# Attention with V stationary and P moving, 1/l and gates in a diagonal operand of P's transposes, on one Trainium2 core

## The reference

```python
def rms_norm_2(x, g):
    y = xf * lax.rsqrt(jnp.mean(xf * xf, axis=-1, keepdims=True) + EPS)
    return (y * g.astype(jnp.float32)).astype(x.dtype)
# NSA, one query block of 128
o_cmp = jnp.einsum('bghtn,bngd->btghd', p_cmp.astype(vc.dtype), vc)
o_slc = jnp.einsum('bghtk,bgtkd->btghd', p.astype(vg.dtype), vg)
o_win = jnp.einsum('bghts,bsgd->btghd', p.astype(vw.dtype), vw)
return g[..., 0:1] * o_cmp + g[..., 1:2] * o_slc + g[..., 2:3] * o_win
# fox
s = jnp.einsum('bthd,bshd->bhts', q[:, lo:hi], k[:, :hi]) * scale
s = s + dcum[:, :, lo:hi, None] - dcum[:, :, None, :hi]
p = masked_softmax(s, jnp.arange(hi)[None, :] <= t[:, None])
outs.append(jnp.einsum('bhts,bshd->bthd', p.astype(v.dtype), v[:, :hi]))
```

## Time and profile before

| | us |
|---|---|
| median of 3 runs | 1473.57 (1469.96 to 1474.71) |
| profiled execution | 1473.89 |
| its span, first to last instruction | 1472.0 |
| mean granted TensorE clock | 0.879 of full |

### The profile page before, as it was taken

The page is one execution under the profiler, slowest core; times in us unless marked ns, Lnnn a source line. Parts: engine busy times, 40 slices in busy tenths (PEclk is TensorE's granted clock), DMA queues, the critical chain, the costliest instruction groups (busy, mean ns, idle before and its releaser), DMA issues. The chain is left out here.

```text
span 1472.0 us, 25094 instructions
## 1 busy us (share of the span) xinstructions
PE 1273.8 (87%) x10545; PEld 1181.0 (80%) x10545; DVE 950.6 (65%) x1742; ACT 647.0 (44%) x1144; POOL 109.9 (7%) x131
## 2 busy tenths in 40 slices
PE   3969886889698977969988889998989889999897
PEld 3967785788677866968966789998989768999897
DVE  2886647566965666566776656888555565688852
ACT  2533222455432224465453345665444344566541
POOL 0121000000110000021000100111011000011100
PEclk9989975799999958989985779999899778999989
DMA  6333200234333002324421034554442502455440
GB/s 254 117 118 137 84 2 1 72 133 158 126 115 110 3 1 104 126 86 170 163 79 54 1 118 151 176 174 170 159 154 90 186 29 77 151 173 173 162 169 29
DMA packets 24449, 167.56 MB, mean 114 GB/s; under 512 B 2705, under 2 KB 2833, under 8 KB 8337
## 3 DMA queue, kind: packets, MB, share of 16 engines
q1 hardware_dynamic: 24336, 165.96, 32.3%
HBM read 164.90 MB, written 1.05 MB: 113 GB/s over the span
## 5 line engine op out<-in xcount | busy, mean ns | idle before, releaser
L395 DVE TENSOR_TENSOR WL<-raw,WH 128x1024 fp32r<-128x1024 f32 (+4 forms) x211 | 243.8, 1176 | 161.5 <-ACT WH L382 161.3
L436 PE MATMUL ps<-FR,WH 128*128 128x256 f32 x1156 | 289.8, 289 | 40.8 <-ACT WH L382 25.6
L438 PE MATMUL ps<-FR,WH 128*128 128x256 f32 x1156 | 284.7, 284 | 1.0 <-POOL FR L508 1.0
L382 ACT ACTIVATE WH<-raw 128x1024 fp32r<-128x1024 f32 (+4 forms) x211 | 203.0, 984 | 131.8 <-PE ps L441 65.3
L436 PEld LDWEIGHTS ps<-FR,WH 128*128 128x128 f32 x1156 | 222.6, 193 | 43.5 <-issue 26.6
L438 PEld LDWEIGHTS ps<-FR,WH 128*128 128x128 f32 x1156 | 222.3, 192 | 3.0 <-POOL FR L508 1.5
L436 PE MATMUL ps<-FR,FR 128*128 128x256 f32 x772 | 199.8, 294 | 16.8 <-ACT FR L504 16.8
L438 PE MATMUL ps<-FR,FR 128*128 128x256 f32 x772 | 198.9, 292 | 2.3 <-DVE FR L508 1.4
L395 DVE TENSOR_TENSOR FR<-raw,FR 128x1024 fp32r<-128x1024 f32 (+2 forms) x114 | 133.9, 1194 | 98.4 <-ACT FR L382 98.4
L436 PEld LDWEIGHTS ps<-FR,FR 128*128 128x128 f32 x772 | 152.6, 198 | 20.0 <-ACT FR L504 15.3
L441 PE MATMUL ps<-FR,WL 128*128 128x256 f32 x1156 | 162.5, 283 | 0.5 <-DVE WL L395 0.5
(11 more groups left out here) (313 smaller groups left out, 1878.1 us busy)
## 6 DMA issues: line engine op xcount, KB each, us to landing
raw<-wst_in SPq DMA_DIRECT2D x123, 1024.0 KB, 4.9
raw<-wst_in SPq DMA_DIRECT2D x17, 896.0 KB, 4.6
raw<-wst_in SPq DMA_DIRECT2D x11, 768.0 KB, 4.2
raw<-wst_in SPq DMA_DIRECT2D x4, 912.0 KB, 4.7
cst<-cst_in SPq DMA_DIRECT2D x1, 1681.0 KB, 13.2
X<-xT_in SPq DMA_DIRECT2D x2, 512.0 KB, 4.4
ARENA<-memT_in SPq DMA_DIRECT2D x1, 1024.0 KB, 4.7
out_dram<-X SPq DMA_DIRECT2D x2, 512.0 KB, 2.6
```

What stands on the lines that cost most here:

```text
L382: a.activation(hi[:, 0:cols], src, ACT.Copy).then_inc(*put("split_hi", ("hi", i)))
L395: v.tensor_tensor(lo[:, 0:cols], src, hi[:, 0:cols].bitcast(F32), SUB).then_inc(*put("split_lo", ("lo", i)))
L436: pe.matmul(out, hv[:, k, :], src.hi[:, c, :], start=k0 == 0 and k == ks[0], stop=False)
L438: pe.matmul(out, hv[:, k, :], src.lo[:, c, :], start=False, stop=False)
```

## The change

1. O is computed with V as the stationary operand (64 columns) and transposed P as the moving one (128 columns), so it comes out feature-major. Two jobs fill the two halves of 64 partitions of one bank, alternately.
2. P's transposes become ordinary fp32 matmuls whose moving operand is `dg`, a 128x128 diagonal of 1/l times the gate, one for each head. DVE builds it (reciprocal, gate multiply, tensor_tensor of the identity and the broadcast row), and T waits for it.
3. The outputs are split at once into `w_o`'s operand: ACT writes the high part ("out hi"), DVE the low one. dil and dsa are multiplied into the gate's place `gd`. The 16 transposes of each `w_o` and the turns of the layers go. In NSA a job is one head with its two branches, and the compressed branch is a third term in the same bank; the POOL adds and `cO` go.
4. Squares are summed on POOL (three adds of 128x512), and a norm takes two matmuls instead of eight.
5. One weight slot less (`NMORE` 3). Steps 0, 1, 3, 4 of compress stand ahead of the NSA turns, the rest between the pairs.

```diff
         if s == 2:
-            qpe.wait_ge(*got("exp", j.id))
+            qpe.wait_ge(*got("dg", j.id))
...
-                    ins = pe.transpose(ps[:, 128 * y:128 * y + 128], j.sm[:, i, 128 * kb:128 * kb + 128], ident)
+                    ins = pe.matmul(ps[:, 128 * y:128 * y + 128], j.sm[:, i, 128 * kb:128 * kb + 128], j.dg[:, min(i, j.nl - 1), :],
+                                    start=True, stop=True)
...
                 for kb in range(nkb):
-                    x = i * nkb + kb
-                    ins = pe.matmul(ps[:, 64 * i:64 * i + 64], j.pt[:, 128 * x:128 * x + 128], j.v(i, kb),
-                                    start=kb == 0, stop=kb == nkb - 1)
-            ins.then_inc(*put("attn_pe", ("O", j.id)))
+                    for p, x in zip(HALVES, (j, j.mate)):
+                        t = 128 * (i * nkb + kb)
+                        ins = pe.matmul(ps[p, o:o + 128], x.v(i, kb), x.pt[:, t:t + 128], start=lead and kb == 0, stop=end and kb == nkb - 1)
+            if "gate" in j.more:
+                for p, x in zip(HALVES, (j, j.mate)):
+                    ins = pe.matmul(ps[p, 0:128], x.more["cmp v"], x.more["cmp p"], start=False, stop=True)
+            ins.then_inc(*put("attn_pe", ("O", j.id), ("O", j.mate.id)))
...
+            v.tensor_tensor(j.dg, bc(ident, 1, j.nl), bc(rl, 2, 128), MUL).then_inc(*put("attn_v", ("dg", j.id)))
+            if j.turn == "V":
+                x, n = j.turns[0]
+                to, ps, free = turn_copy(j, x, n)
...
+                v.tensor_copy(to, ps).then_inc(*put("attn_v", ("pt", j.id, x), free))
...
+                hi, lo = (x[:, c0:c0 + j.n_out, t] for x in (j.parts.hi, j.parts.lo))
+                q.wait_ge(*got("out hi", j.id))
+                v.tensor_tensor(lo, po, hi.bitcast(F32), SUB).then_inc(*put("attn_v", free, *[("lo", j.to, c0 + c) for c in range(j.n_out)]))
...
+    def sum_squares(g_, q, tag, sq, steps=(1, 2, 3)):
+
+        for n in steps:
+            q.wait_ge(*got("square", tag, 2 * n))
+            if n > 1:
+                q.wait_ge(*own("square_sum"))
+            g_.tensor_tensor(sq[0], sq[0], sq[n], ADD).then_inc(*put("square_sum", ("summed", tag, 2 * n)))
...
+            chain = [("compress", 2), ("compress", 5), ("compress", 6), ("compress", 7), (1, 0), (0, 0), (1, 1), (0, 1), (1, 2), (0, 2)]
+            self.steps = chain[0:3] + units[0:2] + chain[3:5] + units[2:6] + chain[5:7] + units[6:10] + chain[7:] + units[10:]
```

More of the change, by code:

```diff
@@ L672, in attn_v @@
         if s == 2:
[L673 to L680, removed]
-            q.wait_ge(*got("exp", j.id))
[L682 to L686, removed]
+            rl = j.st[:, 4:4 + j.nl]
+            q.wait_ge(*got("exp", j.id))
+            if j.sm_before is not None:
+                q.wait_ge(*got("sm free", j.sm_before))
+            v.reciprocal(rl, rl).then_inc(*put("attn_v"))
+            q.wait_ge(*own("attn_v"))
             if "gate" in j.more:
-                q.wait_ge(*got("1/l", j.id))
                 q.wait_ge(*got("gates"))
@@ L729, in attn_a @@
                     a.activation(to, ps, ACT.Copy).then_inc(*put("attn_a", ("pt", j.id, x), free))
-        if s == 3 and j.kind == "dil":
+        if s == 3 and j.mate and "times" not in j.more:
             ps, free = psum("O", j.id)
-            q.wait_ge(*got("1/l", j.id))
+            c0 = j.c0
             q.wait_ge(*got("O", j.id))
[L734 to L743, removed]
+            a.activation(j.parts.hi[:, c0:c0 + j.n_out, 128 * j.b:128 * j.b + 128], ps[:, 0:128 * j.n_out].rearrange("p (c q) -> p c q", c=j.n_out),
+                         ACT.Copy).then_inc(*put("attn_a", ("out hi", j.id), *[("hi", j.to, c0 + c) for c in range(j.n_out)]))
     def rope_v(v, q, tag, zt, H, D, half, cname, sname, TA, TB):
@@ L870, in layer_script @@
         dsa = {b: [[("sel", b, i)] for i in range(7)] + [both("dsa", b, s) for s in range(4)] for b in range(2)}
-        dil = [both("dil", b, s) for b in (1, 0) for s in range(4)] + [[("turn dil",)], [("part dil",)]]
+        dil = [both("dil", b, s) for b in (1, 0) for s in range(4)] + [[("part", 5, 3)]]
         lists = [dsa[1], dil, dsa[0]]
@@ L1414, in layer_pe @@
                 if c0 == 0:
[L1415 to L1416 removed]
+                    mean_mm(("in", l), m.sq[0] if l == 0 else lo_[0].sq3[0])
             elif s[0] == "gate":
@@ L1948, in o_v @@
         barrier(q, "V", stage)
-        split_lo(v, q, "w_o", l, 0, ahead=5)
-        for c in range(8):
-            ps, free = psum("oT", l, c)
-            part_lo(v, q, "part_lo_v", m.Y, ("YO", l), c, ps[:, 0:256], free)
         for c0 in range(0, 8, 2):
@@ L1966, in o_a @@
         barrier(q, "A", stage)
-        split_hi(a, q, "w_o", l, 0, ahead=5)
-        for c in range(8):
-            ps, free = psum("oT", l, c)
-            q.wait_ge(*got("oT", l, c))
-            part_hi(a, m.Y, ("YO", l), c, ps[:, 0:256])
         for c0 in range(0, 8, 2):
@@ L2127, in __init__ @@
             self.cpt = mz.some(2, 3 * 128, "p (h n) -> p h n", h=3)
-            ot2 = mz.some(4, 128, "p (h d) -> p h d", h=2)
-            more = Map(SECOND)
+            more = Map(free)
             sms, pts = sms + more.some(5, 512), pts + more.some(5, 512)
-            slc, win = ([self.job(b, g, i0, kind) for b in (1, 0) for i0 in (0, 2, 4) for g in range(2)] for kind in (0, 1))
-            for n, j in enumerate(win):
-                j.more["add"], j.more["out"] = j.more["out"], ot2[n % 4]
-                j.more["add_before"] = win[n - 4].id if n >= 4 else None
@@ L2155, in __init__ @@
[L2155 to L2164 removed]
+            dgs = Map(zcat).some(4, 256) + Map(tbat + 256).some(3, 256)
@@ L2470, in nsa_g @@
         g_.tensor_tensor(fl(m.Ul), fl(m.U), fl(m.Uh).bitcast(F32), SUB).then_inc(*put("cmp_g", ("Ul",)))
-        for x, s in m.steps:
-            if x not in ("compress", 0, 1):
-                attn_g(g_, q, x, s)
         B.mark("G", "end", "N", "G")
```

345 lines of the change are left out of this document (155 added, 190 removed), and 2 rows, old and new, of the table SEMS.

## The result

| | before | after |
|---|---|---|
| median, us | 1473.82 (1469.96 to 1474.71, 4 runs) | 1553.84 (1550.35 to 1559.43, 4 runs) |
| span of the profiled execution | 1472.0 | 1557.5 |
| mean granted clock | 0.879 | 0.857 |

The changed kernel is slower: ratio 1.0531, 95% interval 1.0493 to 1.0569, +80 us. The forecast was 1497, its range ended at 1524.

The account below looks back on a forecast made before the run. PE was taken to bound most of the kernel, busy 87% of the span. Norms −20, layers −2, fox +21.5 and NSA +24 summed to +23.5 on 1473.9, giving 1497 us; range 1448 to 1524.

Parts of the forecast that it names:

- Part 3: In attention, T waits for DVE's diagonal and alternates with its copy; largest term, fox +21.5 us and NSA +24.
- the signs against it: In the profile after: PE over 85% busy in fox, O at 3.5 us a pair, or clock above 0.9 in both stretches.
- NSA: 0 at full clock, +35 at the lower, taken as +24: NSA attention: chain of 128 us at full clock, 163 at the lower, against 127.7; weighted by a 68% lower-clock share.
- I take 13: NSA's compressed branch: some 40 small DVE operations with PE and ACT steps between, 6 to 17 us, taken as 13.
- Fox: +21.5: Forgetting attention: chain of 61.9 us, 79.4 at the lower clock, against 49.7; +12 to +30, weighted by a 54% share.
- Clock: shares held fixed: Fox and NSA keep their lower-clock shares from before the change, 54% and 68%, giving +21.5 and +24 us.
- −1 each (−4 to +4 together): The two layers: no copy between diagonals; 5 transposed chunks and their multiplies go, 4 multiplies in place come.
- Norms: −20: Mean matmuls: −26 us from fewer records, +3 for POOL at FFN ends, +2.5 ahead of the memory's low parts.
- Part 2: PE work of attention: T doubles, O's halves run abreast, 3.61 to about 1.71 us; pair 7.3 to 7.1, net nothing.
- (b): Rival: three pairs in the weave hide the waits and DVE's own work bounds; 1425 to 1450 us, chance 0.15.
- (c): Rival: O's halves don't run abreast, or the lower clock lasts; +43, 1517 us or 10 to 20 more, chance 0.15.
- (d): Rival: POOL's exposed last adds eat the gain of the mean matmuls, −20 becomes −5; 1512 us, chance 0.10.

Follow-up runs that it names:

- the reordered DVE: Changed kernel with both diagonals of a pair, in NSA and fox, ahead of the copy and the previous pair's low part on DVE: 1474.53 us, ratio 1.0001.
- the first reorder: Changed kernel, but in NSA and fox DVE builds both diagonals of a pair before copying the first job's turn: 1500.53 us, ratio 1.0194.

## Why the prediction was wrong, point by point

The forecast added up to +23.5 us, and the parts as measured give +86.3: 63 us off. In the terms of the sum, some 26 of them are NSA's path, 14 the layers, 9.5 the clock shares, 9.4 the norms and 4.4 fox's path. Each of these parts missed to the same side.

**The direction and the mechanism were right.** Part 3, the serial chain, is what the chain of waits shows, step by step, and undoing it removed the loss. The first wide cycle at the lower clock was put at 10.8 us and measured 10.92: T of a job 1.95 and 2.09, T of its mate 1.71 and 2.07, the diagonal 0.43 and 0.43, copy 0.69 and 0.69, O 1.95 with its end and 1.93 to 2.00. The signs named for this mechanism came: T in two groups, 31 us of idle PE in fox, four L478 records a norm, O of a pair at 1.93 where about 1.7 was named; none of the signs against it came.

**NSA: 0 at full clock, +35 at the lower, taken as +24; measured +55.4. This step failed most.** (134.1 us from the value rows to the first `w_o` matmul, now 189.5.) With the clock share that was measured, 84%, the forecast's own sum gives +29; the other 26 us are path that it left out or put too short:
- Ahead of the first T the sum has 11.4 + 2.1 + 13 + 6.4 = 33 us, up to 2.5 more for the clock. From the end of the value rows (741.9) to the first T (785.36) it is 43.5, 8 more. The products and turns are as forecast (743.80 to 756.8, 13.0 us). The term that was too small is the compressed branch's chain, "I take 13": with the 6.4 it takes 28.6 us (756.8 to 785.36), and PE stands for 1.35, 5.00, 2.76, 1.45 and 3.90 of them in turn.
- The six wide pairs take 73.6 us (785.36 to 858.98), 12.3 each. The forecast had 10.2 at that share and 10.7 with all at the lower clock: 12 more. The first takes 17.2 us. The third term of O (L650, 48 records, 7.0 us of PE in all) stood in no sum, and before one T (825.91) the wait is 3.07 us instead of 1.50: on DVE two maxima (822.53) and two masks (823.85) of newer pairs stand ahead of its diagonal.
- The six narrow pairs (8.1 each where I had at most 7.3) and the two memory pairs take 6 more.

By another cut, the 55.4 are +17.4 in front, +45.2 in the attention and −7.1 in the transition. The transition was as forecast (7 us, all gone). How far each of these terms could be had back was not tried by itself; the reordered DVE took the attention from 157.4 to 103.4 and left the front.

**Fox: +21.5; measured +29.8.** All at the lower clock fox was put at 79.4, and it took 79.5, but at 76% of lower clock, for which the forecast's own sum gives 75.2. So that this one number fits so well is in part luck: of the 8.3 us off, 3.9 are the clock share and 4.4 the path. The three narrow pairs took 23.4 us (1276.57 to 1299.92), where 21.9 was the most.

**Clock: shares held fixed.** "I take the shares of the lower level that these stretches have now, 54% and 68%." They became 76% and 84%. In the sum that is 9.5 us, but the experiments show that the shares are no constant of a stretch: the first reorder alone took busy PE from 1256.5 to 1220.1 us with the same records, at 0.892 instead of 0.857. With the waits before T at 113.7, 89.2, 72.8, 57.6 and 42.2 us, the mean clock of the profiled run was 0.857, 0.892, 0.895, 0.896 and 0.907. That isn't a rule: with the diagonals on POOL there were 71.5 us of waits at 0.884, and the kernel before had 29.5 at 0.879. Which sets which isn't shown by these runs. The two parts of the loss (waits and slower records) can't be summed with the clock held fixed.

**The layers: "−1 each (−4 to +4 together)"; measured +4.7 and +7.0.** The step that failed is "their turns are all ACT's, so no copy stands between the diagonals". True, but I asked only what stands between two diagonals, not what stands ahead of the first: the top-k search. In layer 0 the waits before T grew by 9.9 us (7.55 and 1.82 became 12.70 and 6.60), of which +4.7 is left. A new wait has to be costed by what is queued before it on its engine, in each stage in which it is added.

**Norms: −20; measured −10.6.** The exposure of POOL was mis-sized. I counted 1.5 us at each FFN's end (measured 2.95 − 0.65 = 2.3 and, at the very end, 2.78 − 0.58 = 2.2) and +2.5 for POOL's sums ahead of the memory's low parts (PE's gap there went from 5.1 to 9.9 us, +4.8). With the measured waits the forecast's sum would be −26 + 9.3 = −17; the last 6 us stay open, and the run's own interval is −15 to −6. The bounds given were −14 and −25.

**The slot: 0 to +4.** In the kernel before it costs nothing: ratio 0.996, interval to 0.9986. For that kernel the value taken, 0, was right.

**Part 2, O abreast: right.** 16 records in 1.93 us at the lower clock. The price of tiling changes, which the Trainium skill (TensorEngine Tiling (Array Packing), Key Properties) makes a drain, can't be seen as a loss here: in the chain O starts at 1253.13, where S of another tiling ends, and without the diagonals this kernel, with all its changes of tiling, is 2.85% faster than the one before. Its 8 us stayed in no sum.

**The rivals.** (b), the waits hidden, did not hold in this kernel, where every T waits for DVE. Kernels with another order on DVE come near it: 1454 and 1450, where 1425 to 1450 was forecast. (c), all at the lower clock, was nearest in time and ended at 1517. (d) was right in part: the norms gave −10.6, between −20 and −5. The range, to 1524, hardly reached past the chain as drawn at the lower clock all through; it lacked a longer path in NSA and a loss in the layers and in the norms at the same time.

The sum again with what was measured: −10.6 norms, +11.7 layers, +29.8 fox, +55.4 NSA: +86.3, against +85.5 in the spans.

## What to carry to other kernels

When a product's operand is made just in time by another engine, cost it in that engine's written order: what stands ahead of it there in every stage, and whether a copy that waits for the first product stands ahead of the second operand. Where PE's clock was already low in a stage, the waits were paid more than once here, since the same records ran slower too (24.5 us of waits less came with 36 us of busy PE less); hold no clock share fixed in the sum. Before a rewrite is judged, try the cheap knob on the old kernel: with the cheaper norms, four pairs in flight instead of three gave the old attention as much as the whole new attention had at its best.

## What the runs showed of the hardware

- A power of two floats a partition takes 0.692 us on POOL, a product of 128x256 with a broadcast operand 0.610, a sum of 128x512 1.34 us. On DVE a reciprocal of two takes 0.156 and the 128x256 product 0.424.
- fp32 matmuls with 64 stationary and 128 moving columns into the two halves of a bank: 16 records in 1.93 us in turns, 2.37 to 2.82 one job behind the other, at the lower clock for the most part; all 400 records 44.8 and 60.5 us of busy PE.
- The mean granted clock of the core rose from 0.857 to 0.892 by DVE's order alone, and to 0.907 with another order and four pairs in flight, with the same 10597 records of PE.
